# Reading page numbers block by block, and taking one softmax exponential ahead of a copy, in a two-layer decoder step

## The chip, the cores and the metric

The kernel runs on one core of a Trainium2 chip. It is one launch that holds the whole step. The metric is the device time of the launch in microseconds (us), as the median of several runs.

## The reference

One inference step of a hybrid decoder trunk with two layers: 512 prompt tokens and, beside them, 8 sample sequences of 8 new tokens each, every one with 1024 past tokens in a paged cache (8 pages of 128 rows for each sequence). All is float32. Per layer:

```python
z = x @ w_in                                     # pool, HGRN2, gates, cq, ckv, kpe
y_pool = pool_mixer(...)                         # trailing windows 2, 4, 8, 16
o_hg   = hgrn2(...)                              # gated linear recurrence, 4 heads
past_ckv = cache_ckv[l][page_table].reshape(8, 1024, 128)
past_kpe = cache_kpe[l][page_table].reshape(8, 1024, 32)
s = q_lat . keys_ckv + q_pe . keys_kpe           # 8 heads, causal
o_lat = softmax(s * MLA_SCALE) @ keys_ckv        # attention in latent form
merged = sum_b sigmoid(gate_b) * (branch_b @ w_br_b)
x = layer_norm(alpha * x + merged @ w_out)
x = layer_norm(alpha * x + conv_ffn(x))
```

The part that matters here is the attention of the samples: `past_ckv` and `past_kpe` are gathered through `page_table`, the scores of 64 rows (8 heads x 8 tokens) against 1040 keys are made for each sequence, and then the softmax and the product with the latent rows.

## The kernel before, in words

Every engine has its own instruction list, and semaphores tie them together. A `Fori` loop runs twice over the layers. In a layer come the projections, the attention of the prompt (32 head and block steps, `att_*`), the attention of the samples (`smp_*`), the pool mixer, HGRN2, the gated merge, and the feed-forward part.

The samples are taken in four pairs p = 0 to 3; pair p holds the sequences 2p and 2p + 1. For each pair these steps exist, by engine:

- TensorE: `smp_score(p)` makes the scores. Before its first matmul it waits for both sequences' pages (`page_ready`) and for the pair's rotary keys (`kpe_ready`), 32 DMAs in all. `smp_turn(p)` (L1006, L1010) transposes the probabilities, `smp_values(p)` (L1020, L1023) multiplies them with the latent rows, and `smp_turn_back(p)` (L1032) turns the result.
- VectorE: `smp_stats(p)` (L2226) is the row maximum, `smp_normalise(p)` (L2233, L2235) the scaling, `smp_take_turned(p)` (L2242, L2245) copies the lower half of the turned probabilities and the new keys' part out of PSUM.
- ScalarE: `smp_softmax(p)` (L1776) is the exponential of 128x1040 scores, the "high copy" (by the copy helper, L1613) takes the upper half of the turned probabilities out of PSUM, a further copy takes the product's rows, and `smp_take_cols` the turned result.

TensorE's order is: score(0), the rest of the prompt's attention, score(1); then turn(0), values(0), score(2); turn(1), turn_back(0), values(1), score(3); turn(2), turn_back(1), values(2); turn(3), turn_back(2), values(3), turn_back(3). `smp_values(p)` waits for both VectorE copies and for ScalarE's high copy. After the last pair TensorE goes on with the projections of L893, VectorE with the level differences, and GpSimd, idle until then, with its own part; each waits for the end of the samples' attention.

The sync engine (SP) issues the loads. A page load (`load_page`, L739) brings 128 KB, a load of rotary keys (`load_kpe`, L746) 16 KB. The row of the cache is a number that SP first reads from a table in SBUF into a register (`page_numbers(b)`, L734, eight reads for sequence b; `load_pages`, L753, reads one number ahead of each page). Late in the prompt's attention memory comes free in steps: from half of its scores on for the pages of sequences 5 and 6, from three quarters for the rotary keys of 4 to 7, and after the last for the pages of 7. So SP waits three times on `att_scores`, at L791, L797 and L801. After these loads SP waits for the last product of the samples (L805) and then loads the pool history (L806).

Of the kernel before, what the change touches and what calls it, by code (L numbers as in the profile page):

```python
# [33 lines left out]
N_PAGES = PAST_LEN // PAGE  # L34
# [23 lines left out]
S_PAIRS = DEC_BATCH // 2  # L58
# [118 lines left out]
N_ATT = MLA_HEADS * N_CHUNK  # L177
# [20 lines left out]
def build(nc, xT_in, w_stream, small_in, att_in, const_in, pages_in, kpe_in, page_table, pool_state,  # L198
          hgrn_state, conv_state, yT, ckv_out, kpe_out, pool_out, hgrn_p_out, hgrn_s_out, conv_out):
    with ExitStack() as ctx:  # L200
# [3 lines left out]
        def sem(name):  # L204
# [33 lines left out]
                                                                                    b=DEC_BATCH, h=MLA_HEADS)  # L238
# [163 lines left out]
        def smp_stat(b, which):  # L402

            c = 4 * (N_ATT_BUFS + b % 2) + which
            return stat[:, c:c + 1]
# [58 lines left out]
        def signal(name, per_layer):  # L464
            return Signal(sem(name), per_layer)
# [53 lines left out]
        att_scores = signal("att_scores", N_ATT)  # L519
# [143 lines left out]
        def level_differences(eng, h, first=0, end=len(LEVELS)):  # L663

            for half, out, t0, t1 in levels(h, first, end):
                lo, hi, _ = parts(out, half)
                _, lhi, mid = parts(logf[:, h, t0:t1], half)
                alo, _, _ = parts(log_k[:, h, t0:t1], half)
                mid = mid.broadcast_to([P, (t1 - t0) // (2 * half), half])
                eng.tensor_tensor(hi, lhi, mid, ALU.subtract)  # L670
                ins = eng.tensor_tensor(lo, alo, mid, ALU.add)
            return ins

        def level_scaled(eng, h, first=0, end=len(LEVELS)):

            for half, out, t0, t1 in levels(h, first, end):
                _, hi, _ = parts(out, half)
                _, qhi, _ = parts(q_hg[:, h, t0:t1], half)
                ins = eng.tensor_tensor(hi, hi, qhi, ALU.mult)
            return ins  # L680
# [14 lines left out]
        def _(sp):  # L695
# [5 lines left out]
            def load(l, n, size=LOAD):  # L701

                if n < 2:

                    sp.wait_ge(*down_done.at(l, 1))
                else:

                    sp.wait_ge(*tile_ready.at(l, LAST_TILE[n - 2] + 1))
                load_after(l, n, size)
# [22 lines left out]
            def page_numbers(b):  # L732

                return [sp.value_load(table[0:1, b * N_PAGES + j:b * N_PAGES + j + 1], min_val=0,  # L734
                                      max_val=pages_in.shape[1] - 1) for j in range(N_PAGES)]

            def load_page(l, b, j, n):

                sp.dma_start(page[b][:, j, :],  # L739
                             pages_in[bass.ds(l, 1), bass.ds(n, 1), :, :].rearrange("a b p n -> (a b p) n")  # L740
                             ).then_inc(page_ready[b].sem, 16)

            def load_kpe(l, b, j, n):

                row = 64 * (j // 4) + ROPE * (b % 2)
                sp.dma_start(kpe_pages[b // 2][row:row + ROPE, j % 4 * PAGE:(j % 4 + 1) * PAGE],  # L746
                             kpe_in[bass.ds(l, 1), bass.ds(n, 1), :, :].rearrange("a b p n -> (a b p) n")
                             ).then_inc(kpe_ready[b // 2].sem, 16)
# [13 lines left out]
            with sp.Fori(0, DEPTH) as l:  # L762
# [24 lines left out]
                load_pages(l, 3)  # L787
                for n in range(N_LOADS_PROJ, N_LOADS_PROJ + 2):
                    load(l, n)
                fifth, sixth = page_numbers(5), page_numbers(6)  # L790
                sp.wait_ge(*att_scores.at(l, N_ATT // 2))  # L791
                for j in range(N_PAGES):
                    load_page(l, 5, j, fifth[j])
                for j in range(N_PAGES):
                    load_page(l, 6, j, sixth[j])
                fourth, seventh = page_numbers(4), page_numbers(7)
                sp.wait_ge(*att_scores.at(l, 3 * N_ATT // 4))  # L797
                for b, numbers in ((4, fourth), (5, fifth), (6, sixth), (7, seventh)):
                    for j in range(N_PAGES):
                        load_kpe(l, b, j, numbers[j])  # L800
                sp.wait_ge(*att_scores.at(l, N_ATT))  # L801
                for j in range(N_PAGES):
                    load_page(l, 7, j, seventh[j])

                sp.wait_ge(*smp_pv.at(l, S_PAIRS))  # L805
                sp.dma_start(pool_hist, pool_state[bass.ds(l, 1)].rearrange("o p g b c -> (o p) g b c")  # L806
# [792 lines left out]
        def _(act):  # L1599
# [12 lines left out]
            def copy(out, in_, func=ACT.Copy, **more):  # L1612
                return act.activation(out, in_, func, **more)  # L1613
# [66 lines left out]
            with act.Fori(0, DEPTH) as l:  # L1680
# [89 lines left out]
                def smp_softmax(p):  # L1770
                    s = 4 * (p % 2) * 512
                    act.wait_ge(*smp_max.at(l, p + 1))
                    if p >= 2:
                        act.wait_ge(*smp_turned.at(l, 2 * (p - 1)))
                        act.wait_ge(*smp_recip.at(l, p - 1))
                    act.activation(s_probs[p % 2], ps[:, s:s + S_KEYS], ACT.Exp, bias=smp_stat(p, 0),  # L1776
                                   accum_out=smp_stat(p, 2)).then_inc(smp_exp.sem, 1)

                def smp_take_cols(p):
                    act.wait_ge(*smp_cols.at(l, p + 1))  # L1780
                    copy(o_lat_s[:, :, p * S_NEW:(p + 1) * S_NEW].rearrange("p h (b t) -> p b h t", b=2),
                         back_bank(p).rearrange("p (b h t) -> p b h t", b=2, h=MLA_HEADS)
                         ).then_inc(smp_cols_taken.sem, 1)

                smp_softmax(0)
                for p in range(S_PAIRS):
                    act.wait_ge(*smp_turned.at(l, 2 * p + 2))
                    if p >= 2:
                        act.wait_ge(*smp_pv.at(l, p - 1))
                    copy(s_probs_t[p % 2][:, 4:8, :], bank[7].rearrange("p (j t) -> p j t", j=4)  # L1790
                         ).then_inc(smp_high_taken.sem, 1)
                    if p < S_PAIRS - 1:
                        smp_softmax(p + 1)
                    if p >= 1:
                        smp_take_cols(p - 1)
                    act.wait_ge(*smp_pv.at(l, p + 1))
                    if p >= 1:
                        act.wait_ge(*smp_cols.at(l, p))
                    copy(s_out_rows, bank[3][:, 0:P]).then_inc(smp_rows.sem, 1)
# [1287 lines left out]
```

## Time and profile before

| | us |
|---|---|
| median of 3 runs | 2285.3 |
| lowest and highest | 2284.06, 2288.4 |
| the profiled execution, its own time | 2288.4 |
| its span, first to last instruction | 2286.6 |
| TensorE matmul busy | 2205.3 (96% of the span) |
| VectorE, ScalarE, GpSimd busy | 1169.6, 514.3, 994.8 |
| mean granted TensorE clock | 0.989 |

The samples' attention lies from about 210 to 248 us in the first layer and from about 1345 to 1382 us in the second. The times in the trace are us from the start of the span. "Busy" is time in which an engine's instruction ran; the matmuls' ends are modelled. The chain of work is followed back from the last instruction, at each step to what released it. A float32 matmul or transpose shows as two records. SP's own reads, register steps and waits are not in the timeline, only its DMA issues; its reads are found under their line.

### The profile page before, as it was taken

Reading aid. Unit: us, or ns where it says so; the run is one execution under the profiler, and the core shown is the slowest. Engines: PE = TensorE matmul, PEld = TensorE weight load, DVE = VectorE, ACT = ScalarE, POOL = GpSimd, SP = SyncE. Lnnn points to the kernel's source line nnn. Section 1 sums busy time; section 2 is a strip of 40 time slices with the busy share of each in tenths; the row PEclk is TensorE's granted clock in tenths of the full one; section 3 lists DMA queues with packets and bytes.
Section 4 is the critical chain, followed back from the end, with each engine's and each line's share of the span. In section 5 each row is a group of like instructions: output and inputs, shape, how many; then the busy total and the mean of one; then the engine's idle time right before and its main releaser. Section 6 shows DMA issues by size and latency. Waiting matters only on the chain.

```text
span 2286.6 us, 36930 instructions
## 1 busy us (share of the span) xinstructions
PE 2205.3 (96%) x11856; PEld 1697.2 (74%) x11856; DVE 1169.6 (51%) x2116; ACT 514.3 (22%) x1088; POOL 994.8 (44%) x1128
## 2 busy tenths in 40 slices
PE   8999999999989999999899999999999899999996
PEld 6776777777767777777676757777777677777775
DVE  0544666333576666661226346743335666666522
ACT  1434353111131100100134343531111311100002
POOL 0000046667655666633300001465676466666251
PEclk9999999999999999999999999999999999999998
DMA  5322113222132222222132221132221222221211
GB/s 206 102 84 66 42 63 113 84 75 83 47 125 74 73 73 73 85 72 76 38 132 83 76 66 42 63 131 68 80 84 56 106 78 88 73 73 68 94 54 42
DMA packets 51616, 183.54 MB, mean 80 GB/s; under 512 B 7234, under 2 KB 27970, under 8 KB 37762
## 3 DMA queue, kind: packets, MB, share of 16 engines
q1 hardware_dynamic: 50882, 178.49, 22.7%
q10 hardware_dynamic: 576, 3.06, 0.3%
q8 instruction: 84, 1.38, 0.2%
q14 instruction: 74, 0.61, 0.1%
HBM read 172.35 MB, written 9.18 MB: 79 GB/s over the span
## 4 chain that ended last, share of the span: by engine, by line
PE 91%; DVE 4%; issue 2%; ACT 1%; POOL 1%; SPq 1%; DMA 0%; DVEq 0%; ACTq 0%
PE ps L1214 25%; PE ps L1134 21%; PE ps L1252 16%; PE ps L893 12%; PE ps L1503 3%; PE ps L1417 2%; PE ps L925 1%; PE ps L1282 1%; PE ps L946 1%; PE ps L934 1%; PE ps L914 1%; PE ps L1074 1%; DVE xT L2084 1%; PE ps L978 1%; PE ps L1020 1%
## 5 line engine op out<-in xcount | busy, mean ns | idle before, releaser
L1214 PE MATMUL ps<-lq,mreg 128*128 128x288 f32 x1008 | 251.3, 406 | 0.0
L893 PE MATMUL ps<-xT,wring 128*128 128x288 f32 (+2 forms) x960 | 238.2, 411 | 2.9 <-DMA wring<-w_stream 1.5
L1214 PEld LDWEIGHTS ps<-lq,mreg 128*128 128x128 f32 x1008 | 191.5, 190 | 52.9
L1613 ACT ACTIVATE r<-ps 128x288 f32<-128x288 f32 (+8 forms) x272 | 114.0, 425 | 505.8 <-PE ps L1134 256.4
L893 PEld LDWEIGHTS ps<-xT,wring 128*128 128x128 f32 x960 | 184.4, 192 | 55.2 <-issue 2.2
L1214 PE MATMUL ps<-xT,wring 128*128 128x288 f32 x672 | 169.8, 406 | 0.0
L1214 PEld LDWEIGHTS ps<-xT,wring 128*128 128x128 f32 x672 | 127.7, 190 | 35.3
L1134 PE MATMUL ps<-r,kbuf 128*128 128x288 f32 x576 | 143.6, 406 | 0.0
L1134 PEld LDWEIGHTS ps<-r,kbuf 128*128 128x128 f32 x576 | 109.4, 190 | 30.2
L2737 POOL TENSOR_TENSOR kbuf<-o_mla 128x288 f32<-128x288 f32 x42 | 33.3, 793 | 219.9 <-DVE o_mla L2511 219.9
L1928 ACT ACTIVATE r<-r 128x592 f32<-128x592 f32 x44 | 30.7, 697 | 428.1 <-DVE r L2548 427.8
L1613 ACT ACTIVATE o_mla<-ps 128x288 f32<-128x288 f32 (+1 forms) x108 | 45.4, 421 | 337.4 <-PE ps L1252 214.5
L2636 POOL TENSOR_TENSOR mreg<-vbuf,const 64x512 f32<-64x512 f32 x8 | 8.3, 1035 | 253.4 <-PE ps L1531 244.7
L2764 POOL TENSOR_TENSOR kbuf<-kbuf,lq 128x2304 f32<-128x2304 f32 x2 | 10.1, 5054 | 249.2 <-DVE side L2191 249.2
L2548 DVE SCALAR_TENSOR_TENSOR r<-r,small 128x592 f32<-128x592 f32 x88 | 104.7, 1189 | 12.4 <-DVE r L2545 12.1
L2545 DVE SCALAR_TENSOR_TENSOR r<-r,small 128x592 f32<-128x592 f32 x88 | 104.5, 1187 | 12.4 <-DVE r L2542 10.3
L1134 PE MATMUL ps<-xT,wring 128*128 128x288 f32 x384 | 97.0, 406 | 0.0
L1252 PE MATMUL ps<-r,side 128*128 128x288 f32 x372 | 92.7, 407 | 0.8 <-DVE r L2559 0.8
L1214 PE MATMUL ps<-xT,mreg 128*128 128x288 f32 x336 | 88.3, 406 | 0.0
L1214 PE MATMUL ps<-lq,wring 128*128 128x288 f32 x336 | 88.3, 406 | 0.0
L1134 PEld LDWEIGHTS ps<-xT,wring 128*128 128x128 f32 x384 | 73.0, 190 | 20.2
L1134 PE MATMUL ps<-lq,r 128*128 128x288 f32 x336 | 87.3, 406 | 0.0
(429 smaller groups left out, 4523.6 us busy)
## 6 DMA issues: line engine op xcount, KB each, us to landing
wring<-w_stream SPq DMA_DIRECT2D x100, 1024.0 KB, 4.9
side<-w_stream SPq DMA_DIRECT2D x18, 704.0 KB, 4.4
r<-pages_in SPq DMA_DIRECT2D x80, 128.0 KB, 2.2
vbuf<-w_stream SPq DMA_DIRECT2D x12, 512.0 KB, 3.7
r<-w_stream SPq DMA_DIRECT2D x12, 512.0 KB, 3.6
wring<-w_stream SPq DMA_DIRECT2D x8, 704.0 KB, 4.1
r<-w_stream SPq DMA_DIRECT2D x6, 704.0 KB, 4.2
mreg<-pages_in SPq DMA_DIRECT2D x32, 128.0 KB, 2.1
```

The costliest lines, as they stand in the source:

```text
L893: mm = pe.matmul(out[0:w.shape[-1], a * 512:a * 512 + hi - lo], w, x[:, lo:hi], start=(k == 0), stop=(k == len(pairs) - 1))
L914: mm = pe.matmul(slot(tile + j)[:, a * 512:a * 512 + hi - lo], w, xT[:, k, lo:hi], start=(k == 0), stop=(k == KD - 1))
L1134: mm = pe.matmul(banks[name], ws[:, k * P:(k + 1) * P], xs[:, k, :], start=(k == 0), stop=(k == n - 1))
L1214: mm = pe.matmul(up_sum[name], ws[:, k * P:(k + 1) * P], xs[:, k, :], start=(k == 0), stop=(k == HK - 1))
L1252: mm = pe.matmul(res_bank(which, m, i - 1), ws[:, k * P:(k + 1) * P], x, start=(k == 0), stop=(k == len(xs) - 1))
L1417: mm = pe.matmul(bank[2 * x + a][:, 0:HALF], w, xT[:, k, a * HALF:(a + 1) * HALF], start=(k == 0), stop=(k == KD - 1))
L1503: mm = pe.matmul(slot(TILE_HI + m)[g:g + rows, part * 256:(part + 1) * 256], xT[:, k, m * P:m * P + rows], w_slot[part][:, k * 256:(k + 1) ...
L1613: return act.activation(out, in_, func, **more)
L1928: act.activation(conv_h[u][0][:, 0:CX - 2], conv_h[u][0][:, 0:CX - 2], ACT.Silu).then_inc(silu_done.sem, 1)
L2545: dve.scalar_tensor_tensor(out=out, in0=src[:, 1:CX - 1], scalar=scalar(col + 2 * KF), in1=out, op0=ALU.mult, op1=ALU.add).then_inc(conv_s ...
L2548: dve.scalar_tensor_tensor(out=out, in0=src[:, 2:CX], scalar=scalar(col + 4 * KF), in1=out, op0=ALU.mult, op1=ALU.add).then_inc(conv_done. ...
L2737: pool.tensor_tensor(up_v[u], up_u2[u], up_p5s[u], ALU.add).then_inc(up_v_ready.sem, 1)
```

## The change

It has two parts. On SP, the page numbers are no longer read for two sequences together and kept; each block of eight loads has its own eight reads just ahead of it, the numbers of sequences 5 and 6 are read a second time for their rotary keys, and for sequence 7 the pages and the rotary keys are issued alternately, both after the last wait. On ScalarE, the exponential of pair 1 is issued right after that of pair 0, ahead of the first high copy. In the loop, p = 0 has no exponential any more.

```diff
-                fifth, sixth = page_numbers(5), page_numbers(6)
-                sp.wait_ge(*att_scores.at(l, N_ATT // 2))
-                for j in range(N_PAGES):
-                    load_page(l, 5, j, fifth[j])
-                for j in range(N_PAGES):
-                    load_page(l, 6, j, sixth[j])
-                fourth, seventh = page_numbers(4), page_numbers(7)
-                sp.wait_ge(*att_scores.at(l, 3 * N_ATT // 4))
-                for b, numbers in ((4, fourth), (5, fifth), (6, sixth), (7, seventh)):
+                for b in (5, 6):
+                    numbers = page_numbers(b)
+                    if b == 5:
+
+                        sp.wait_ge(*att_scores.at(l, N_ATT // 2))
                     for j in range(N_PAGES):
+                        load_page(l, b, j, numbers[j])
+                for b in (4, 5, 6, 7):
+                    numbers = page_numbers(b)
+                    if b == 4:
+
+                        sp.wait_ge(*att_scores.at(l, 3 * N_ATT // 4))
+                    elif b == 7:
+
+                        sp.wait_ge(*att_scores.at(l, N_ATT))
+                    for j in range(N_PAGES):
+                        if b == 7:
+                            load_page(l, b, j, numbers[j])
                         load_kpe(l, b, j, numbers[j])
-                sp.wait_ge(*att_scores.at(l, N_ATT))
-                for j in range(N_PAGES):
-                    load_page(l, 7, j, seventh[j])
...
                 smp_softmax(0)
+                smp_softmax(1)
                 for p in range(S_PAIRS):
...
-                    if p < S_PAIRS - 1:
+                    if 1 <= p < S_PAIRS - 1:
                         smp_softmax(p + 1)
```

## Rows read from the trace of the kernel before

**Rows 1.** The page: the chain that ended last, shares of the span.

```profile
PE 91%; DVE 4%; issue 2%; ACT 1%; POOL 1%; SPq 1%; DMA 0%; DVEq 0%; ACTq 0%
```

**Rows 2.** The chain in order of time, 205 to 250 us: start, us, what.

```profile
225.22 1.87 PE ps L978 x8
...
230.72 1.90 PE ps L1020 x32
232.62 0.36 PE ps L1023 x4
232.98 1.87 PE ps L978 x8
```

**Rows 3.** Timeline of SP's DMA issues, first layer: start, us from first to last issue.

```profile
179.24 10.22 SPq L739 DMA_DIRECT2D r<-pages_in  x16
198.57 18.97 SPq L746 DMA_DIRECT2D r<-kpe_in  x32
217.83 4.34 SPq L739 DMA_DIRECT2D r<-pages_in  x8
245.93 0.33 SPq L806 DMA_DIRECT2D r<-pool_state  x1
```

**Rows 4.** The same, second layer.

```profile
1314.42 9.62 SPq L739 DMA_DIRECT2D r<-pages_in  x16
1333.16 19.18 SPq L746 DMA_DIRECT2D r<-kpe_in  x32
1352.64 4.33 SPq L739 DMA_DIRECT2D r<-pages_in  x8
```

**Rows 5.** Who SP waited for: us in total, times, longest.

```profile
SPq L806 <- PE ps L1023: 45.8, 2, 23.5
...
SPq L739 <- PE ps L926: 22.8, 2, 11.4
```

**Rows 6.** Line L734, 175 to 200 us: ns min/median/max, first to last start.

```profile
L734 SPq TENSOR_LOAD <-table x16: 265/266/275, 189.5 to 197.7; - x16
```

**Rows 7.** Line L739, 198 to 225 us.

```profile
L739 SPq DMA_DIRECT2D r<-pages_in x8: 332/333/354, 217.8 to 221.8; - x8
...
DMA to landing us min/median/max: 2.1/2.1/2.3
```

**Rows 8.** Line L746, 198 to 218 us.

```profile
L746 SPq DMA_DIRECT2D r<-kpe_in x32: 315/316/840, 198.6 to 217.2; - x32
...
DMA to landing us min/median/max: 1.5/1.7/2.4
```

**Rows 9.** Timeline of pair 0 and pair 1, first layer; in brackets idle before.

```profile
219.10 1.24 DVE L2226 TENSOR_REDUCE stat<-ps 128x1 f32<-128x1040 f32 x1 [0.97 <-PE ps L996]
...
220.14 0.60 ACT L1613 ACTIVATE r<-ps 128x512 f32<-128x512 f32 x1 [3.00 <-PE ps L1010]
...
220.63 1.12 ACT L1776 ACTIVATE r<-ps,stat 128x1040 f32<-128x1040 f32 x1
220.86 0.27 DVE L2245 COPY s_new_t<-ps 16x128 f32<-16x128 f32 x1
...
221.27 3.43 PE L1020 MATMUL ps<-r 128*64 128x128 f32 x32 [1.18 <-DVE s_new_t L2245]
221.64 0.20 ACT L1776 ACTIVATION_READ_ACCUMULATOR r<-ps,stat 128x1 f32 x1
...
222.07 0.76 DVE L2235 TENSOR_SCALAR r<-r,stat 128x1040 f32<-128x1040 f32 x1
...
228.72 1.07 PE L1006 MATMUL ps<-const,r 128*128 128x128 f32 x8
...
232.91 1.94 PE L978 MATMUL ps<-r,side 128*64 128x512 f32 x8
```

**Rows 10.** Timeline of TensorE, second layer.

```profile
1356.49 1.97 PE L1020 MATMUL ps<-r 128*64 128x128 f32 x32 [1.18 <-DVE s_new_t L2245]
...
1366.52 1.94 PE L978 MATMUL ps<-r,side 128*64 128x512 f32 x8
```

**Rows 11.** Who TensorE waited for: us in total, times, longest.

```profile
PE ps L1417 <- ACT xT L1677: 12.1, 2, 6.1
```

**Rows 12.** Stretches: length, busy PE, PEld, DVE, ACT, POOL, granted clock, DMA share, GB/s.

```profile
221.60:224.90 3.30, 3.30 (x33) 2.97 (x30) 0.93 (x2) 0.24 (x2) 0.00 (x0) 0.50 0.41 126
...
675.00:682.00 7.00, 2.67 (x6) 1.98 (x7) 7.00 (x11) 5.07 (x6) 4.25 (x4) 0.54 0.85 317
...
1356.50:1360.00 3.50, 3.50 (x42) 2.39 (x44) 0.92 (x2) 0.84 (x3) 0.00 (x0) 1.00 0.40 121
```

## The prediction

> **What bounds the kernel now.** I read the page first. The chain that ended last is TensorE's for 91% of the span [rows 1], so a part of the change counts if it moves TensorE. The next view is the same chain inside the samples' attention [rows 2]: there TensorE goes from the product of pair 1 (230.72, 232.62) straight into the scores of pair 3 (232.98). Nothing stands between them, so the loads of pair 3 were there in time. How early they were is the question for the first part of the change, and SP's issues, its waits and the landing times answer it. The second part is read from the timeline of pairs 0 and 1 [rows 9].
>
> SP first. After the wait for half of the prompt's scores it issues 16 pages from 179.24 on, 32 rotary loads from 198.57 on, and 8 pages from 217.83 to 222.17 [rows 3]. Between the first two groups lie 9.1 us (189.46 to 198.57), and they are filled by 16 reads of page numbers, from 189.5 on, one every (197.7 - 189.5) / 15 = 0.547 us [rows 6]. Of the three waits on the prompt's scores (their matmul is L926) the list of SP's waits holds only the first, two times and 11.4 us each [rows 5]; it has no row of L926 for the rotary loads and no third and fourth time for the pages. So from 179.24 to 222.17 SP is never waiting: it is a full queue of reads and issues, and every step added to it moves its end by its own length.
>
> The last page is issued at 221.8 and lands 2.1 us later [rows 7], at 223.9. TensorE wants it at 232.91, the first matmul of score(3) [rows 9]. Spare time in the first layer: 9.0 us. In the second layer the last issue starts at 1352.64 + 4.33 - 0.33 = 1356.64 [rows 4], lands at 1358.7, and is wanted at 1366.52 [rows 10]: 7.8 us to spare.
>
> **The change, SP's part.** The DMAs stay the same 56 per layer (24 pages, 32 rotary loads). What changes is the number of reads behind the first wait. Before, 16 (sequences 4 and 7). After: the numbers of 6, which stood ahead of the wait and were free there; those of 4; those of 5 and of 6 a second time; those of 7. That is 40, so 24 more, at 0.547 us: 13.1 us. None of this is covered, since SP does not wait between. Up to the first rotary load nothing moves: 16 pages and 16 reads before, 16 pages and 16 reads after. Sequences 4 and 5 come 4.4 us later at most (eight more reads) and are wanted by score(2) at about 225.2 [rows 2], long after the 16th rotary load (half of the 32, near 208 [rows 3]). So pair 2 is safe and the whole 13.1 us falls on pair 3.
>
> The last DMA is now a rotary load, which lands after 1.7 us [rows 8] where a page takes 2.1. The price per issue stays: a page issue comes every (221.8 - 217.8) / 7 = 0.57 us [rows 7], a rotary one every (217.2 - 198.6) / 31 = 0.60 [rows 8]. The 0.60 holds some longer issues (up to 840 ns where the median is 316 [rows 8]). Without any long one, at a median of 0.55 for rotary loads and 0.57 for pages, the 56 issues would take about 31.3 us where they take 10.22 + 18.97 + 4.34 = 33.5 and some tenths at the seams; so if the reads between the blocks let the queue breathe and all long issues vanish, SP gains about 3 us back. I keep them in, because the long ones come in the blocks of pages (16 in 10.22 us, 0.66 each, against 0.57 [rows 3, 7]) and of rotary loads alike, and take the 3 us as the lower bound.
>
> Score(3) therefore starts later by
> - first layer: 13.1 - 9.0 - 0.4 = 3.7 us,
> - second layer: 13.1 - 7.8 - 0.4 = 4.9 us.
>
> What is behind it: turn(2) and everything of TensorE; VectorE's and ScalarE's work for pairs 2 and 3 waits for that; SP's L806 waits for the last product, with 23.5 us of waiting in hand [rows 5]. All engines meet at the end of the samples' attention, so nothing later takes the delay in. It goes to the end of the kernel in full: 8.6 us.
>
> The Trainium skill speaks against this ("DMA: Bandwidth & Descriptors", section "Issuing engines are not separate DMA queues"): the time of the sequencer to start a DMA is usually small beside the DMA itself. By that rule SP's part would be free and the sum would be ScalarE's part alone. The trace disagrees: 56 issues and 16 reads fill 42.9 us of the queue, where one landing is 2.1.
>
> **The change, ScalarE's part.** Before, the high copy of pair 0 ran at 220.14 for 0.60, and the exponential of pair 1 at 220.63; its maximum was ready at 219.10 + 1.24 = 220.34 [rows 9]. Now the exponential is first: it starts at about 220.4, its accumulator read 1.01 later, and the high copy about 0.1 after that, at 221.5. It ends at 222.1. The product of pair 0, which started at 221.27, released by VectorE's copy of 220.86 + 0.27 = 221.13 (so 0.14 after its releaser), now waits for the high copy: 222.1 + 0.14 = 222.2, which is 0.95 us later. Gain: the exponential is 0.25 us earlier, and so the scaled probabilities of pair 1. They were ready at 222.83 and are wanted by turn(1) at 228.72 [rows 9], after score(2) in TensorE's order; 5.9 us early already, so the gain is nothing. The second layer has the same order and the same idle time of 1.18 before that product [rows 10].
>
> So ScalarE's part alone costs 0.95 x 2 = 1.9 us. But in front of score(3) stands SP's stream, whose end does not depend on it: TensorE comes to score(3) 0.95 later and waits 0.95 less. Where the loads are late by more than 0.95, this cost is not added.
>
> **The clock.** TensorE will idle 3.7 - 0.95 = 2.8 us and 4.9 - 0.95 = 3.9 us in front of score(3). In the trace the long waits (6.1 us at L1417 [rows 11]) have a granted clock of 0.54 about them (1.2 GHz for nearly all of it), and after the 1.18 us of idle time before values(0) it was 0.50 in the first layer and 1.00 in the second [rows 12]. The same 32 matmuls took 3.43 us at the one and 1.97 at the other [rows 9, 10]; with the four that follow a fall cost about 1.6 us. The loss of the first layer's fall at values(0) goes into the wait, as above. Behind each new wait I expect a fall, part of which lies in the idle time itself; between 0 and 1.6, I take 1.2 for each, 2.4 together, as the idle times lie between the two rows.
>
> The Trainium skill has it the same way round ("TensorE: Matmul & The Clock Gate", "What's actually happening"): half rate is the default, and activity releases it; a rule without those falls would leave the sum at 8.6.
>
> **Sum.** 8.6 + 2.4 = 11.0 us. Against the profiled execution's own time of 2288.4 this is 2299.4; that one was the slowest of three, 3.1 above the median of 2285.3. Against the median: 2296.3 us, 0.48% slower. What a measurement of this kernel can tell from no change is about 0.2%, 4.6 us.
>
> **Rivals.**
> - *The added reads do not lengthen SP's list* (not slower). If numbers that are read twice were kept and not read again, 8 reads or 4.4 us would be added, under the 7.8 and 9.0 us to spare, and only ScalarE's 1.9 us would be left: 2287.2. It decides where fewer than 14 of the 24 reads are really paid in the second layer (7.8 / 0.547). For it: the trace has no number read twice. Against: every read written shows as an own TENSOR_LOAD. 9%. The rule of the Trainium skill on the sequencer's time, above, would end at the same 2287.2.
> - *The long issues vanish.* SP's end is 3 us earlier: first layer 0.7, so ScalarE's 0.95 counts; second 4.9 - 3.0 = 1.9; with a fall in each layer at values(0), now 2.1 us idle, or at score(3), 0.5 to 3 us: about 5, so 2290.5. For it: reads between the blocks thin out the queue. Against: 16 reads ahead of the rotary block did not keep long issues out of it. 15%.
> - *No fall of the clock.* 8.6 alone, 2293.9. The 1.18 us of the second layer passed without. 14%.
> - *Faster.* The earlier exponential would have to be what turn(1) waits for; it is 5.9 us early. Or the first layer's fall at values(0) disappears without a new one: 1.6 less, with the loads in time, 2285.6, which is no change. 3% for over 0.2%.
>
> **How the numbers follow.** The main case has 55%, its own range 2294 to 2299. With the rivals (9, 15, 14), 3% for faster and 4% for something worse than both full falls (8.6 + 3.2 is 2297.1), the range for 8 in 10 goes from the vanished long issues with one small fall, 2289, to the main case on a slow execution, 2300. Slower by over 0.2% (above 2289.9): 55 + 14 + 4 and two thirds of the 15, so 83%. Within: 14%. Faster: 3%.
>
> **What would show it.** SP's timeline: after the first 16 pages and reads the first rotary load at about 198.6 as before, the last load at about 235 (first layer), with five groups of eight reads under L734 behind the first wait. TensorE: score(3) at L978 with 3 to 4 us of idle time before it, released by a DMA of rotary keys; values(0) 0.95 later with ScalarE's copy as releaser. The forecast is wrong if SP's reads get cheaper than 0.547, if score(3) shows no idle time, or if the time behind the samples' attention takes the delay in.

## The result, and the profile after

The changed kernel takes 2298.49 us (median of 6 runs, 2296.12 to 2302.74) where the kernel before took 2284.68 in the same comparison (2282.38 to 2288.40). The ratio is 1.0059, with a 95% interval of 1.0046 to 1.0073: 13.5 us slower by the ratio (the medians differ by 13.8). Forecast were 11.0 us and 2296.3.

The page of the changed kernel names SP in the chain that ended last, with 4% of the span where [rows 1] has 1%. Its span is 2298.5 us, its own time 2300.27.

```profile
PE 87%; SPq 4%; DVE 3%; issue 3%; ACT 1%; POOL 1%; DMA 1%; DVEq 0%; ACTq 0%
```

Who TensorE waited for, in the changed kernel (us in total, times, longest). The scores are now L983, the products L1025. Both rows are new.

```profile
PE ps L983 <- DMA r<-kpe_in: 6.6, 2, 4.3
...
PE ps L1025 <- ACT r L1618: 4.2, 2, 2.1
```

The timeline of SP's issues in the changed kernel, first layer, which answers to [rows 3].

```profile
178.27 13.64 SPq L739 DMA_DIRECT2D r<-pages_in  x16
196.65 22.21 SPq L746 DMA_DIRECT2D r<-kpe_in  x24
223.58 0.35 SPq L739 DMA_DIRECT2D r<-pages_in  x1
224.17 0.33 SPq L746 DMA_DIRECT2D r<-kpe_in  x1
...
230.39 1.68 SPq L739 DMA_DIRECT2D r<-pages_in  x1
...
233.44 0.32 SPq L746 DMA_DIRECT2D r<-kpe_in  x1
250.88 0.34 SPq L811 DMA_DIRECT2D r<-pool_state  x1
```

Line L734 in the changed kernel, 176 to 224 us (reads behind the first wait; [rows 6] has 16).

```profile
L734 SPq TENSOR_LOAD <-table x40: 262/267/276, 182.6 to 222.8; - x40
```

The chain in order of time, 205 to 260 us, of the changed kernel, which answers to [rows 2].

```profile
233.44 1.99 DMA r<-kpe_in
235.56 3.68 PE ps L983 x8
239.24 1.56 PE ps L988 x8
```

Read together they say this. SP issues from 178.27 to 233.76 without a wait, with 40 reads in between, and the last rotary load lands 1.99 us after its issue. TensorE had ended the product of pair 1 by 231.3 and stood until 235.56. The chain steps from TensorE onto that DMA and from there onto SP's list. The matmuls that follow take 3.68 us where the same eight records took 1.94 in [rows 9]: the clock was at 1.2 GHz.

SP's wait ahead of the first page load of sequence 5, in the changed kernel (us in total, times, longest), which answers to the second line of [rows 5]:

```profile
SPq L739 <- PE ps L931: 31.6, 2, 15.8
```

Each time it is 15.8 us where it was 11.4: eight reads (4.4 us) that stood ahead of this wait, inside its time, now stand behind it.

### The profile page after: what moved, and what is told of

Same layout as the page of the kernel before. It is cut to its first block, busy times and chain, and to the rows that moved or that the text cites. A ratio compares the mean times of both kernels' runs of the same rounds, so it can differ in the third digit from the quotient of the medians.

```text
span 2298.5 us, 37026 instructions
## 1 busy us (share of the span) xinstructions
PE 2208.8 (96%) x11856; PEld 1697.5 (74%) x11856; DVE 1172.8 (51%) x2116; ACT 514.2 (22%) x1088; POOL 993.2 (43%) x1128
## 4 chain that ended last, share of the span: by engine, by line
PE 87%; SPq 4%; DVE 3%; issue 3%; ACT 1%; POOL 1%; DMA 1%; DVEq 0%; ACTq 0%
PE ps L1219 25%; PE ps L1139 21%; PE ps L1257 16%; PE ps L898 12%; PE ps L1508 3%; SPq L734 2%; PE ps L1422 2%; SPq L746 1%; PE ps L1287 1%; SPq L739 1%; PE ps L930 1%; PE ps L919 1%; PE ps L1079 1%; DVE xT L2090 1%; PE ps L1409 1%
## 5 line engine op out<-in xcount | busy, mean ns | idle before, releaser
L2554 DVE SCALAR_TENSOR_TENSOR r<-r,small 128x592 f32<-128x592 f32 x88 | 104.6, 1189 | 12.4 <-DVE r L2551 12.0
L2551 DVE SCALAR_TENSOR_TENSOR r<-r,small 128x592 f32<-128x592 f32 x88 | 104.5, 1188 | 12.4 <-DVE r L2548 10.6
```

The costliest lines, as they stand in the source:

```text
L2551: dve.scalar_tensor_tensor(out=out, in0=src[:, 1:CX - 1], scalar=scalar(col + 2 * KF), in1=out, op0=ALU.mult, op1=ALU.add).then_inc(conv_s ...
L2554: dve.scalar_tensor_tensor(out=out, in0=src[:, 2:CX], scalar=scalar(col + 4 * KF), in1=out, op0=ALU.mult, op1=ALU.add).then_inc(conv_done. ...
```

## The experiments

All positions in this table are us from the first page load of sequence 5, so that a difference ahead of this stretch does not count (in the changed kernel that load is at 178.27 and 1319.62, before at 179.24 and 1314.42). "Reads" are those behind the first wait. The two numbers are first and second layer. The ratio is to the kernel before, with its 95% interval.

| kernel | reads | last load issued | score(3) starts | idle before it | ratio |
|---|---|---|---|---|---|
| before | 16 | 42.6, 42.2 | 53.7, 52.1 | 0, 0 | 1 |
| before, second trace | 16 | 42.6, 42.3 | 52.1, 52.1 | 0, 0 | |
| changed | 40 | 55.2, 53.9 | 57.3, 57.0 | 4.3, 2.3 | 1.0059 (1.0046 to 1.0073) |
| SP's part | 40 | 54.7, 54.5 | 56.5, 56.3 | 4.4, 4.2 | 1.0053 (1.0039 to 1.0067) |
| SP's part, 5 and 6 kept | 24 | 46.0, 46.2 | 52.1, 52.1 | 0, 0 | 0.9994 (0.9985 to 1.0003) |
| SP's part, 16 read again | 32 | 51.1, 51.2 | 54.2, 54.3 | 2.1, 2.1 | 1.0030 (1.0019 to 1.0042) |
| order alone | 16 | 44.2, 42.3 | 53.7, 52.1 | 0, 0 | 1.0009 (1.0000 to 1.0019) |
| before with 24 reads more | 40 | 57.6, 57.3 | 60.1, 59.7 | 8.0, 7.5 | 1.0079 (1.0064 to 1.0095) |
| before with 48 reads more | 64 | 71.0, 69.8 | 73.4, 72.3 | 19.6, 20.1 | 1.0192 (1.0176 to 1.0207) |

The same for ScalarE's part; the positions are those of the product of pair 0.

| kernel | product starts | idle before it | 32 matmuls took | ratio |
|---|---|---|---|---|
| before | 42.0, 42.1 | 1.18, 1.18 | 3.43, 1.97 | 1 |
| changed | 43.0, 43.0 | 2.09, 2.09 | 1.97, 3.05 | 1.0059 |
| ScalarE's part | 43.0, 43.0 | 2.09, 2.09 | 1.97, 2.99 | 1.0024 (1.0012 to 1.0036) |
| ScalarE's part, second trace | 43.0, 43.0 | 2.09, 2.09 | 1.97, 2.72 | |
| change with 5 and 6 kept | 43.0, 43.0 | 2.09, 2.09 | 1.97, 2.54 | 1.0024 (1.0015 to 1.0033) |
| scores of pair 2 first | 44.4, 44.5 | 0, 0 | 1.97, 1.97 | 0.9992 (0.9982 to 1.0002) |
| the same with ScalarE's part | 44.5, 44.5 | 0, 0 | 1.97, 1.97 | 0.9984 (0.9975 to 0.9993) |

**ScalarE's part alone.**

```diff
                 smp_softmax(0)
+                smp_softmax(1)
...
-                    if p < S_PAIRS - 1:
+                    if 1 <= p < S_PAIRS - 1:
                         smp_softmax(p + 1)
```

> The kernel before with ScalarE's part of the change alone. Theory (SP's queue of reads and issues makes the loss, and ScalarE's part hides in front of the same wait): the product of pair 0 starts 0.9 us later in each layer, released by ScalarE's copy, score(3) follows the product of pair 1 without idle time, and the kernel takes 1.9 us more, 2286.6, a ratio of 1.0008, within what can be told from no change. Rival (the exponential put first is what costs most, by the clock that falls behind the longer idle time): 5 us or more, ratio 1.002 or above.

The direct cost came as expected: the product of pair 0 starts 0.91 us later, behind ScalarE's copy. This is TensorE's timeline in the second layer of this kernel.

```profile
1353.59 2.99 PE L1020 MATMUL ps<-r 128*64 128x128 f32 x32 [2.09 <-ACT r L1613]
1356.50 0.69 PE L1023 MATMUL ps<-r,s_new_t 16*64 16x128 f32 x4
```

But the ratio is 1.0024, 5.5 us, and its interval (2.7 to 8.2 us) leaves 1.9 out. Taken by its ratio, the rival's number is met. The trace does not show where all of it goes: it is of an execution of 2284.43 us, the fastest of this kernel's eight, whose median is 2289.76. What it does show is given below.

**SP's part alone.** Its diff is the first part of the change.

> The kernel before with SP's part alone. Theory: the end of SP's queue does not depend on ScalarE, so score(3) starts as late after the first page load of sequence 5 as in the changed kernel (57.3 us in the first layer, 57.0 in the second), the idle time in front of it is about 1 us longer (about 3.7 and 4.9 if the clock does not fall ahead of it), and the time is that of the changed kernel, ratio 1.0055 to 1.006. Rival (the two parts add up): 1.9 us less than the changed kernel, ratio 1.0050, with the idle time in front of score(3) as in the changed kernel.

Score(3) starts 0.6 to 0.8 us earlier than in the changed kernel, since the last load was issued earlier by 0.5 us in the first layer and landed sooner in the second (1.7 us after its issue, where it was 2.9 in the changed kernel). So without ScalarE's part it is not late by less than the loads are: the idle time is 4.4 and 4.2 us here. TensorE's timeline in its first layer:

```profile
234.55 3.68 PE L983 MATMUL ps<-r,side 128*64 128x512 f32 x8 [4.38 <-DMA r<-kpe_in]
238.16 1.98 PE L988 MATMUL ps<-r,side 32*64 32x512 f32 x8
```

The ratios 1.0053 and 1.0059 don't tell the theory from the adding up of 1.9 us; the positions speak for the theory. So does the length of the samples' attention, from the first page load of sequence 5 to the first matmul of the projections behind it: 67.4 us in each layer in the second trace of the kernel before, 74.9 and 73.9 in the changed kernel (14.0 more), 74.6 and 74.3 with SP's part alone (14.1 more). ScalarE's part adds nothing to it. ScalarE's part alone (5.5 us) and SP's alone (12.1 us) sum to 17.6, above the changed kernel's 13.5, as far as such intervals can say.

**SP's part without the second reading.**

```diff
+                kept = {}
                 for b in (5, 6):
-                    numbers = page_numbers(b)
+                    numbers = kept[b] = page_numbers(b)
...
                 for b in (4, 5, 6, 7):
-                    numbers = page_numbers(b)
+                    numbers = kept[b] if b in kept else page_numbers(b)
```

> SP's part, but the numbers of sequences 5 and 6 are kept and not read again: 24 reads behind the first wait where the kernel before has 16 and the changed one 40. Theory: 8 reads are 4.4 us, under the 9.0 and 7.8 us to spare; no idle time in front of score(3), ratio 1.000. Rival (the new order of the loads or the alternation of pages and rotary keys costs, not the reads): still slower by several us, ratio above 1.003.

As the theory said: 0.9994, and no idle time in front of the scores. The loads stand in the order of the changed kernel here, 7's alternating, so that order costs nothing. TensorE's timeline in the first layer:

```profile
229.63 1.97 PE L1026 MATMUL ps<-mreg,r 128*64 128x128 f32 x32
231.52 0.43 PE L1029 MATMUL ps<-r,s_new_t 16*64 16x128 f32 x4
231.89 1.51 PE L984 MATMUL ps<-r,side 128*64 128x512 f32 x6
```

**SP's part with 16 numbers read again, those of 6 also ahead of the wait.**

```diff
+                ahead = {b: page_numbers(b) for b in (5, 6)}
                 for b in (5, 6):
-                    numbers = page_numbers(b)
+                    numbers = ahead[b]
```

> SP's part, but the numbers of 6 are read ahead of the first wait as before, and those of 5 and 6 are read a second time: 32 reads behind the first wait, 16 more than before, 8.8 us. Theory: 8.8 - 9.0 - 0.4 is below nothing in the first layer and 8.8 - 7.8 - 0.4 = 0.6 us in the second; with up to one fall of the clock 0 to 2.5 us more, ratio 1.000 to 1.001. Rival (a loss in proportion to the added reads, two thirds of 13.5): 9 us, ratio 1.004.

A miss: 1.0030 is 6.9 us. The reads cost what they should (the last issue is 8.5 and 9.0 us later than before). But the last load landed 3.0 us after its issue, not 1.7, and in the first layer the spare time was not 9.0 us, as no fall of the clock had held TensorE up. So score(3) is late by 2.1 us in the first layer and 2.2 in the second. The second layer had a fall behind the wait (1.7 us more), the first had none: 6.0 us by the trace. The interval holds the rival's 1.0040 too; what speaks against a loss in proportion to the reads is the kernel above, where 8 more of them cost nothing.

```profile
1369.69 3.63 PE L984 MATMUL ps<-r,side 128*64 128x512 f32 x8 [2.14 <-DMA r<-kpe_in]
1373.25 1.09 PE L989 MATMUL ps<-r,side 32*64 32x512 f32 x8
```

**24 and 48 reads put into the kernel before.** Three or six such lines stand ahead of the last wait; their values are not used.

```diff
+                page_numbers(4)
+                page_numbers(5)
+                page_numbers(6)
                 sp.wait_ge(*att_scores.at(l, N_ATT))
```

> The kernel before with 24 reads of page numbers put in, all in one place between the rotary loads and the last wait; order of the loads and ScalarE as before. Theory (it is the number of reads in SP's list, wherever they stand): the last page load is issued 55.5 us after the first of sequence 5, lands 2.1 later, score(3) starts at 57.7 where it is 52.1 without a fall of the clock ahead of it; with falls behind the wait ratio 1.0055 to 1.007. Rival (it is the order of the loads, or the numbers kept in registers): ratio 1.000.

> The same with 48 reads. Theory: every further read costs its 0.547 us in full once the spare time is used up: score(3) starts 13.1 us later than with 24, at about 70.8, in each layer, 26.3 us more in all; ratio 1.018. The falls of the clock cost no more than with 24, since one is at most as long as the wait makes it. Rival (loss in proportion to the reads from the first on): twice the loss with 24, ratio about 1.012.

The reads alone make the loss, with the order of the loads and ScalarE untouched. From 24 to 48 the start of score(3) moves by 13.3 and 12.6 us, against 13.1 for 24 reads. The ratio moves by 0.0113, 25.8 us for 48 reads, 0.54 us each; 26.3 were expected. The rival is out: twice the loss with 24 would be 1.0158, below the interval. With 24 it was 1.0079, above the expected range: SP's list got 15 us longer, not 13.1. The reads took 13.3 of it. Long issues among its 56 add up to 3.7 and 3.3 us beyond 0.33 each, where the kernel before has 2.3 and 1.9 and SP's part 1.0 and 0.8. Of the kernel with 48 more, TensorE's first layer and a stretch of it (length, busy PE, PEld, DVE, ACT, POOL, granted clock, DMA share, GB/s):

```profile
252.51 3.40 PE L984 MATMUL ps<-r,side 128*64 128x512 f32 x8 [19.61 <-DMA r<-pages_in]
```

```profile
235.10:252.40 17.30, 0.00 (x0) 0.00 (x0) 0.00 (x0) 0.00 (x0) 0.00 (x0) 0.50 0.20 61
252.60:255.40 2.80, 2.80 (x8) 0.74 (x8) 0.00 (x0) 0.00 (x0) 0.00 (x0) 0.50 0.00 0
```

Every engine stands for 17 us while SP reads, and the clock is low when the work comes back.

**The order of the loads alone.** The pages and rotary keys of 7 are issued alternately behind the last wait, with the numbers as before.

```diff
-                for b, numbers in (..., (7, seventh)):
+                for b, numbers in (...):
...
                 for j in range(N_PAGES):
                     load_page(l, 7, j, seventh[j])
+                    load_kpe(l, 7, j, seventh[j])
```

> The kernel before, with the pages and the rotary keys of sequence 7 issued alternately and nothing else; the same 16 reads behind the first wait. Theory: the last load is issued within 1 us of before, no idle time in front of score(3), ratio 1.000. Rival (alternation of two kinds of load makes issues long): the last issue several us later.

No idle time in front of the scores. The last issue is 1.6 us later in the first layer, more than expected and far inside the spare time. The ratio is 1.0009 (1.0000 to 1.0019), near no change: 2.1 us, of which the trace shows none in front of score(3).

**The whole change without the second reading.** The two diffs above together.

> The whole change, but the numbers of sequences 5 and 6 are kept and not read again (24 reads behind the first wait). Theory: SP's part then costs nothing and ScalarE's part shows as it does alone, with 2.09 us of idle time in front of the product of pair 0: ratio 1.002 to 1.003, and no idle time in front of score(3). Rival (the two parts need each other to cost): ratio 1.000.

1.0024, as with ScalarE's part alone: with 24 reads instead of 40 behind the wait, SP's part is gone and ScalarE's shows.

**The scores of pair 2 ahead of the product of pair 0.**

```diff
+                    if p == 0:
+                        smp_score(l, 2)
                     smp_values(l, p)
-                    if p + 2 < S_PAIRS:
-                        smp_score(l, p + 2)
+                    if p == 1:
+                        smp_score(l, 3)
```

> The kernel before with one step of TensorE moved: the scores of pair 2 are made ahead of the product of pair 0, not behind it. The product then no longer follows 1.18 us of idle time; about 0.75 us of idle time should appear in front of the turn of pair 1 instead, since that waits for the copy of the product's rows. Theory (clock falls follow idle time there): about 0.4 us less per layer and fewer falls, ratio 0.9990 to 1.000. Rival (no effect of the idle time on the clock): ratio 1.000 to within 0.05%.

> The same with ScalarE's part of the change as well. Theory (ScalarE's part costs only by the longer idle time in front of the product of pair 0, 0.92 us directly and the rest of its 1.0024 by more frequent falls of the clock behind it): the high copy ends before TensorE wants the product, so nothing is left of it: the same ratio as with the step of TensorE alone, within 0.1%. Rival (taking the exponential first costs by itself, through VectorE's or ScalarE's later work): again about 0.2% more than that kernel.

The idle time in front of the product is gone, and 0.47 us (0.75 were expected) stand ahead of the turn of pair 1. Score(3) starts at 51.4 where 52.1 is the start before without a fall. The kernel with TensorE's step alone is at 0.9992, which is not told from 1. With ScalarE's part as well it is 0.9984, and this interval ends below 1: 2282.62 us against 2285.67. It is the only one of these kernels whose interval does so, and the two intervals overlap. So no cost of ScalarE's part is left once TensorE has other work. In the timeline of that kernel the copy ends 1.6 us before the product starts:

```profile
221.49 1.13 ACT L1778 ACTIVATE r<-ps,stat 128x1040 f32<-128x1040 f32 x1 [3.24 <-DVE stat L2229]
...
222.61 0.59 ACT L1615 ACTIVATE r<-ps 128x512 f32<-128x512 f32 x1
...
224.80 1.97 PE L1020 MATMUL ps<-r 128*64 128x128 f32 x32
```

**Second traces of ScalarE's part and of the kernel before.**

> A second look at ScalarE's part alone. Theory (after 2.09 us of idle time the clock falls more often than after 1.18): at least one of the two layers shows a fall within the product of pair 0, and the time is 2284 to 2294. Rival (falls there are as rare as in the kernel before): none in either layer.

> A second look at the kernel before, for how often the clock falls within the product of pair 0 after 1.18 us of idle time. Theory: in none or one of the two layers; where it does not fall, score(3) starts 52.1 us after the first page load of sequence 5. Rival: a fall in both.

Over all traces with 1.18 us of idle time ahead of the product of pair 0, 3 of 16 products ran with a fallen clock (each time the first layer's). With 2.09 us it was 4 of 8 (each time the second layer's). A fall there holds up what follows by 1.6 us (the product of pair 1 starts at 52.3 instead of 50.7). Both expectations were met: the second trace of ScalarE's part, of 2288.53 us, has one fall at the product, and that of the kernel before has none, with score(3) at 52.1. The counts are too few to show that falls are more frequent after the longer idle time.

## Why the prediction was right, and where its sizes were off

**SP is a full queue; reads behind the wait are paid in full: right, shown.** 24 added reads moved the last issue by 12.6 and 11.7 us, forecast 13.1. The dose runs give 0.54 us each against the 0.547 read from [rows 6], and taking 16 of them away took the loss away. The little that is missing are mostly shorter long issues (1.5 and 0.2 us in the changed kernel, 2.3 and 1.9 before), which the forecast had as its lower bound. In the four kernels that read the numbers of 6 between the pages of 5 and of 6 these add up to at most 1.5 us per layer, in all others to 1.7 or more, so reads at that place go with fewer of them; why is not shown. The kernel with 24 reads in one place has 3.7 and 3.3.

**Score(3) late by 3.7 and 4.9 us: right against the profiled execution, mis-sized against the median.** Measured from the first page load, it starts 3.6 and 4.85 us later. That both agree so closely is in part luck. In the second layer the last load was issued 1.4 us earlier than forecast, and the landing, put at 1.7 us, took 2.9, which gave most of that back:

```profile
1373.52 0.32 SPq L746 DMA_DIRECT2D r<-kpe_in  x1
```

```profile
1376.57 3.34 PE L983 MATMUL ps<-r,side 128*64 128x512 f32 x8 [2.30 <-DMA r<-kpe_in]
```

In the first layer it was 0.5 us earlier and landed after 2.0. The term of -0.4 for the landing was thus wrong: it was -0.1 in the first layer and +0.9 in the second. And the 9.0 us to spare in the first layer came from an execution in which the clock had fallen at the product of pair 0 [rows 12] and held TensorE up by 1.6 us. Without it score(3) is at 52.1 in both layers and about 7.4 us are to spare. That fall came in only 3 of 16 products. So for a usual execution the step should have been 5.2 and 4.9 us (57.3 and 57.0 against 52.1).

**A fall of the clock behind each wait: right; 1.2 us each was too little.** From score(3) to the product of pair 2 it is 5.50 us at 2.4 GHz. In the changed kernel it is 7.78 and 7.13, so 2.3 and 1.6 us; in SP's part alone 2.8 and 2.6. These are stretches of the changed kernel behind the first and the second wait.

```profile
235.60:240.20 4.60, 4.60 (x16) 1.09 (x16) 0.00 (x0) 0.00 (x0) 0.00 (x0) 0.50 0.00 0
...
1377.00:1380.30 3.30, 3.30 (x12) 0.90 (x12) 0.00 (x0) 0.00 (x0) 0.00 (x0) 0.50 0.00 0
```

The upper bound of 1.6 was taken from the one low stretch at the product; after 4.3 us of idle time the low stretch lasted for 4.8 us of work (235.56 to about 240.3). The Trainium skill's account ("TensorE: Matmul & The Clock Gate", "What's actually happening"), that activity releases the half rate, agrees with the direction: the granted clock was 0.50 when the work began and 1.00 from 240.4 on.

**The sum.** By the traces: 3.6 + 2.3 in the first layer and 4.85 + 1.6 in the second make 12.4 us against a span that grew by 11.9 (the changed kernel's first page load was 0.97 us earlier). With 1.6 us for the fall that the first layer of before usually lacks it is 14.0, and the ratio says 13.5. Of the 3.0 us that the forecast of 11.0 is below these 14.0, 1.6 are that fall and 1.5 the falls behind the waits (2.3 + 1.6 where 2.4 stood).

**ScalarE's part: the mechanism was right, its stand-alone price was not.** The product starts 0.9 us later as forecast (0.95), and in front of SP's wait this is swallowed: score(3) starts 0.14 us after the last load has landed, with and without ScalarE's part. In the second layer of the changed kernel even a fall at that product was: the wait behind it was 2.3 us instead of 3.9. Alone it costs 5.5 us, not 1.9. More frequent falls would give 0.3 x 2 x 1.6 = 1.0 us by the counts above. The rest, some 2.6 us, is inside the ratio's interval but is not shown to be anything. In both traces of ScalarE's part alone the samples' attention takes 68.3 and 69.9 us where it took 67.4 and 67.4: 0.9 us in the first layer, 2.5 with a fall in the second, 3.4 in all. The other 2.1 us of the 5.5 can't be placed: from the first layer's samples' attention to the second layer's first page load, two traces of one kernel differ by 2.3 to 2.6 us. The two kernels with the scores of pair 2 first show that the cost goes when the product no longer waits for the high copy; how much of it was the wait and how much the clock stays open.

**Nothing later takes the delay in: right.** From the end of the samples' attention to the second layer's first page load the two traces differ by 0.3 us, and from the second layer's to the end by 0.2. With 48 reads more, where the delay is some 45 us, both are still within 0.5 us of the kernel before.

**The rule on issue time** of the Trainium skill ("DMA: Bandwidth & Descriptors", "Issuing engines are not separate DMA queues"), that the sequencer's time is usually small beside the DMA's, holds here for a single load (0.33 us to issue, 1.7 to 2.1 from issue to landing) but not for this list: the reads and issues of 56 loads of 16 and 128 KB set when the last one lands.

## What to carry to other kernels

A queue that shows no wait between its first and last issue is a resource with a price per step: find the consumer of its last transfer, measure the time to spare, and multiply the steps added behind its last real wait by that price. A register read there costs as much as an issue (0.547 us against 0.55 to 0.60 here), and ahead of a wait that is longer than the reads it costs nothing. When spare time is read from one execution, look whether the clock had fallen ahead of the consumer, for then it is larger than usual.

## What the runs showed of the hardware that was not expected

- The landing of the last small load varied: 1.7 us at the median, 2.0 and 2.9 in the two layers of the changed kernel and 3.0 in both of the kernel with 16 numbers read again. What it depends on is not shown.
- Some DMA issues on SP take up to 1.8 us where 0.33 is usual. Over 56 issues the excess was 0.2 to 4.0 us, and it differed between two traces of the same kernel (about 2.4 and 4.0 in the first layer of ScalarE's part).
- The granted clock stayed at 0.50 over 17.3 us without work, and for the first 2.8 us of work after it.
